# PEER's rows of u turned by VectorE in 32x32 squares, with plain fp32 products beside the picking and split products behind it

## The reference, cut to what matters

```python
def peer_ffn(h, q_w, sub_keys, u_tab, v_tab):      # h: 256 x 1024, u_tab, v_tab: 16384 x 1024
    q = (t @ q_w).reshape(n, 8, 2, 128)
    s = jnp.einsum('thpd,hpnd->thpn', q, sub_keys)           # 8 heads, 2 x 128 keys
    s1, i1 = lax.top_k(s[:, :, 0], 16)
    s2, i2 = lax.top_k(s[:, :, 1], 16)
    ...                                                      # 16 of the 256 sums of a head
    gates = jax.nn.softmax(top_s, axis=-1)
    act = jax.nn.gelu(jnp.einsum('chkd,cd->chk', u_tab[i_c], x_c))
    return jnp.einsum('chk,chkd->cd', g_c * act, v_tab[i_c])
```

## Time and profile before

| | us |
|---|---|
| median of 3 runs | 2324.53 |
| lowest and highest | 2319.58, 2325.33 |
| the profiled execution | 2319.86 |
| its span | 2318.1 |

### The profile page before, as it was taken

How to read it: one execution, slowest core, us unless ns; L and a number is a source line. 1 busy time by engine, 2 the same in 40 slices (tenths; PEclk the granted TensorE clock), 3 DMA queues, 4 the chain that set the end, 5 groups by cost and what they waited for, 6 DMA issues and landing times.

```text
span 2318.1 us, 37450 instructions
## 1 busy us (share of the span) xinstructions
PE 2145.5 (93%) x14407; PEld 1931.0 (83%) x14407; DVE 1409.6 (61%) x2315; ACT 1016.8 (44%) x1870; POOL 186.9 (8%) x217
## 2 busy tenths in 40 slices
PE   6999899878899999789999699999999999999997
PEld 6876788778788889778888599999999999777775
DVE  5435777677676752154434628997666654666665
ACT  4443443458553343233333424443444444555554
POOL 2101000001000000300000000000223341000000
PEclk9999999999999999879999899999999999999998
DMA  7543566734657743300001333343333335555553
GB/s 254 184 172 110 190 218 220 245 117 160 221 166 267 252 158 131 83 1 1 1 1 37 109 111 128 128 137 119 115 113 114 115 119 175 189 190 190 190 190 136
DMA packets 157432, 333.74 MB, mean 144 GB/s; under 512 B 17382, under 2 KB 69340, under 8 KB 157160
## 3 DMA queue, kind: packets, MB, share of 16 engines
q1 hardware_dynamic: 153896, 321.18, 41.0%
q0 software_dynamic: 3392, 10.52, 1.3%
HBM read 330.58 MB, written 1.08 MB: 143 GB/s over the span
## 4 chain that ended last, share of the span: by engine, by line
PE 73%; DVE 12%; PEld 7%; ACT 3%; issue 3%; SPq 1%; DMA 1%; PEldq 1%; DVEq 0%; ACTq 0%
PE psum L2130 18%; PE psum L2131 17%; PE psum L2132 17%; PE psum L2652 4%; PE psum L2699 2%; PEld psum L2130 2%; PEld psum L2131 2%; PEld psum L2132 2%; DVE weights_lo L1493 2%; PE psum L2542 2%; PE psum L2548 2%; DVE u_lo L2080 1%; PE psum L2523 1%; ACT weights_hi L1037 1%; PE psum L2428 1%
## 5 line engine op out<-in xcount | busy, mean ns | idle before, releaser
L1493 DVE TENSOR_TENSOR weights_lo<-weights,weights_hi 128x1024 fp32r<-128x1024 f32 (+2 forms) x336 | 345.3, 1085 | 260.4 <-ACT weights_hi L1037 255.3
L2130 PE MATMUL psum<-input_hi,weights_hi 128*128 128x256 f32 x1288 | 370.9, 288 | 19.0 <-DVE weights_lo L1493 6.1
L1037 ACT ACTIVATE weights_hi<-weights 128x1024 fp32r<-128x1024 f32 (+2 forms) x336 | 289.2, 931 | 178.7 <-PEq L2177 117.5
L2131 PE MATMUL psum<-input_lo,weights_hi 128*128 128x256 f32 x1288 | 367.1, 285 | 0.0
L2132 PE MATMUL psum<-input_hi,weights_lo 128*128 128x256 f32 x1288 | 366.9, 285 | 0.0
L2130 PE MATMUL psum<-input_hi,u_hi 128*128 128x256 f32 x1024 | 299.8, 293 | 0.0
L2132 PE MATMUL psum<-input_hi,u_lo 128*128 128x256 f32 x1024 | 289.3, 283 | 0.0
L2131 PE MATMUL psum<-input_lo,u_hi 128*128 128x256 f32 x1024 | 289.2, 282 | 0.0
L2130 PEld LDWEIGHTS psum<-input_hi,weights_hi 128*128 128x128 f32 x1288 | 250.0, 194 | 34.6 <-issue 32.7
L2080 DVE TENSOR_TENSOR u_lo<-psum,u_hi 128x512 fp32r<-128x512 f32 x256 | 164.8, 686 | 167.4 <-ACT u_hi L1419 165.9
L2131 PEld LDWEIGHTS psum<-input_lo,weights_hi 128*128 128x128 f32 x1288 | 250.0, 194 | 0.0
(11 more groups left out here) (376 smaller groups left out, 4001.4 us busy)
## 6 DMA issues: line engine op xcount, KB each, us to landing
u_rows<-in_peer_u_dram SPq DMA_DIRECT2D x128, 512.0 KB, 3.4
weights<-in_ffn_w_in_dram SPq DMA_DIRECT2D x44, 1024.0 KB, 7.3
v_rows_even<-in_peer_v_dram SPq DMA_DIRECT2D x64, 512.0 KB, 3.5
v_rows_odd<-in_peer_v_dram SPq DMA_DIRECT2D x64, 512.0 KB, 3.4
weights<-in_ret_w_in_dram SPq DMA_DIRECT2D x24, 1024.0 KB, 7.3
ada_rows_in<-in_ada_w_dram SPq DMA_DIRECT2D x24, 1024.0 KB, 5.2
weights<-in_ffn_w_out_dram SPq DMA_DIRECT2D x44, 512.0 KB, 6.5
weights<-in_lru_w_in_dram SPq DMA_DIRECT2D x12, 1024.0 KB, 6.3
```

Source lines behind the costliest of these rows:

```text
L1037: nc.scalar.activation(whi[:, r, at_], wraw[:, r, at_], ACT.Copy).then_inc(s_whi[r], 1)
L1493: ins = nc.vector.tensor_tensor(wlo[:, r, at_], wraw[:, r, at_], whi[:, r, at_].bitcast(F32), ALU.subtract)
L2130: nc.tensor.matmul(o, ah, bh, start=start, stop=False)
L2131: nc.tensor.matmul(o, ah, bl, start=False, stop=False)
```

## The change

SyncE loads a block of u in four DMAs of 32 rows each, so that partition 32a + e holds features 256a to 256a + 255 of row e; a transpose of every 32x32 square by VectorE then gives chunks of 128 features by 128 experts. A chunk k holds the features 256a + 32k + j, so the input of PEER is brought in the same order: `modulate` writes the second of its two instructions in that order, and the query weights' rows are loaded to match, one DMA for each chunk (8 a slot). TensorE's transposes of u are gone. For blocks 0 to 48 (`PARTED`) the turned rows go straight to plain fp32 products, 8 a block, with an unsplit input `HT` that GpSimd adds up from `HH` and `HL`; they use four buffers. From block 49 on ScalarE and VectorE split the turned rows, in one instruction of 1024 each, out of SBUF. The one-hot rows of both factors are made by one instruction, and the gate is multiplied into them by ScalarE (`gates_in`, four instructions) in place of VectorE.

```diff
+PARTED = GROUP_FIRST
+def plain_buffer(j):
+    return j % 4
+def parted(j):
+    return (j - PARTED) // 2 + 1
...
         UR = low.take("u_rows", [P, 2, D])
+        HT = Region("u's hi parts, before", low.at, 8 * KB).take("input_t", [P, KT, S])
         UTH = low.take("u_hi", [P, 2, KT, P], F32R)
+        UF2 = Region("u's lo parts, before", low.at, 8 * KB).take("u_turned_more", [P, 2, KT, P])
         UTL = low.take("u_lo", [P, 2, KT, P], F32R)
+        UT = Region("idle rows", rows_at, 8 * KB).take("u_turned", [P, 2, KT, P])
+        UF = [UT[:, 0], UT[:, 1], UF2[:, 0], UF2[:, 1]]
...
+                for k in range(KT):
+                    sp.dma_start(wraw[:, r, k * BANK:(k + 1) * BANK], q_rows[k, :, :, j * BANK:(j + 1) * BANK])\
+                        .then_inc(s_wload[r], 16)
...
-                sp.dma_start(UR[:, b, :], u_tab[bass.ds(i * 256 + j * P, P), :]).then_inc(s_ur[b], 16)
+                for c in range(4):
+                    four = u_tab[bass.ds(i * 256 + j * P + c * 32, 32), :].rearrange("e (a k) -> a e k", a=4)
+                    sp.dma_start(UR[:, b, c * 256:(c + 1) * 256], four).then_inc(s_ur[b], 16)
...
+                nc.gpsimd.tensor_tensor(HT[:, half, :], HH[:, half, :].bitcast(F32), HL[:, half, :].bitcast(F32), ALU.add)\
+                    .then_inc(s_ht, 1)
...
             def u_high(j):
+                if j < PARTED:
+                    return
+                b = j % 2
+                act.wait_ge(s_ut[b], j // 2 + 1)
+                act.wait_ge(s_ap, max(j - 1, PARTED))
+                nc.scalar.activation(UTH[:, b, :, :], UT[:, b, :, :], ACT.Copy).then_inc(s_uh[b], 1)
+
+            def gates_in(g):
+                act.wait_ge(s_oh, g + 1)
+                for x in range(4):
+                    one = ONE[:, g % 2, 0, x, :]
+                    t = 4 * g + x
+                    ins = nc.scalar.activation(one, one, ACT.Copy, scale=HKT[:, 2, t:t + 1])
+                ins.then_inc(s_ohg, 1)
...
                 if group_made(j - 2) is not None:
                     gates_out(group_made(j - 2), j + 1)
+                if group_made(j) is not None:
+                    gates_in(group_made(j))
...
+                if j < 2 and isinstance(i, int):
+                    act.wait_ge(s_ul[j], parted(P - 2 + j))
...
+            def turn_u(j):
+                b = j % 2
+                dve.wait_ge(s_ur[b], 64 * (j // 2) + 64)
+                if j < PARTED:
+                    dst = UF[plain_buffer(j)]
+                    if j >= 4:
+                        dve.wait_ge(s_ap, j - 3)
+                else:
+                    dst = UT[:, b]
+                    if j < PARTED + 2:
+                        dve.wait_ge(s_ap, max(m for m in range(j) if m < PARTED and plain_buffer(m) == b) + 1)
+                    else:
+                        dve.wait_ge(s_ul[b], parted(j - 2))
+                nc.vector.transpose(dst.rearrange("p k (c e) -> p c k e", c=4),
+                                    UR[:, b, :].rearrange("p (c k j) -> p c k j", c=4, k=KT)).then_inc(s_ut[b], 1)
+
             def u_low(j):
+                if j == 0:
+                    turn_u(0)
+                if j + 1 < P:
+                    turn_u(j + 1)
+                if j >= PARTED:
+                    b = j % 2
+                    dve.wait_ge(s_uh[b], parted(j))
+                    nc.vector.tensor_tensor(UTL[:, b, :, :], UT[:, b, :, :], UTH[:, b, :, :].bitcast(F32), ALU.subtract)\
                         .then_inc(s_ul[b], 1)
...
-                nc.vector.tensor_tensor(ONE2[:, half, :], iota, of(1), ALU.is_equal)
-                chain.done(nc.vector.tensor_tensor(ONE1[:, half, :], iota, of(0), ALU.is_equal))
-                nc.vector.tensor_tensor(ONE1[:, half, :], ONE1[:, half, :], of(2), ALU.mult).then_inc(s_oh, 1)
+                nc.vector.tensor_tensor(ONE[:, g % 2], iota, places, ALU.is_equal).then_inc(s_oh, 1)
...
+                if j < PARTED:
+                    pe.wait_ge(s_ut[b], j // 2 + 1)
+                    for k in range(KT):
+                        ins = nc.tensor.matmul(PS[:, 2 + b, 0:S], UF[plain_buffer(j)][:, k, :], HT[:, k, :],
+                                               start=k == 0, stop=k == KT - 1)
```

More of the change, by code:

```diff
@@ L355, with slot_loads @@
 GROUP_FIRST = len(PICKS) + 3
+PARTED = GROUP_FIRST
[3 more added lines that the diff above has]
+    return (j - PARTED) // 2 + 1
+def slot_loads(s0, use):
+    late = s0 - SLOTS["peer_q"]
+    return 32 * use + 32 if late < 0 else 32 * (use - late // 2) + 16 * KT * (late // 2 + 1)
 def group_made(j):
@@ L555, in first_and_second_block @@
         NS = Region("idle input", hh_at + 8 * KB, 8 * KB).take("na_scores", [P, 4, 512])
+        NP = Region("idle input", hh_at + 8 * KB, 8 * KB).take("scaled", [P, TT, D])
         NPT = Region("low-rank inputs", lora_at, 4 * KB).take("na_probs_t", [P, 2, 512])
@@ L639, in first_and_second_block @@
         s_oh = sem("s_oh")
+        s_ohg = sem("s_ohg")
+        s_ht = sem("s_ht")
         s_ur = [sem(f"s_ur{b}") for b in range(2)]
@@ L996, in _ @@
             load_rows(14, 18)
+            for u in range(4):
+                evacuated(UNITS["norm_p"] + u)
+            for j in (2, 3):
+                r, use = slot(SLOTS["peer_q"] + j)
+                pool.wait_ge(s_wlo[r], use + 1)
+            for h in range(2):
+                half = slice(4 * h, 4 * h + 4)
+                nc.gpsimd.tensor_tensor(HT[:, half, :], HH[:, half, :].bitcast(F32), HL[:, half, :].bitcast(F32), ALU.add)\
+                    .then_inc(s_ht, 1)
             def gate_block(j):
@@ L1553, in gain_row, with modulate @@
                 return dst
-            def modulate(src, scale):
+            def modulate(src, scale, turned=False):
                 shift = row()
+                lies = (lambda x: x.rearrange("p (a k j) -> p a k j", a=4, k=KT)) if turned else lambda x: x
                 for tt in range(TT):
                     inverse_rms(tt)
-                    chain.done(nc.vector.scalar_tensor_tensor(XS[:, tt, :], src[:, tt, :], rs[:, tt:tt + 1], scale,
+                    scaled = (NP if turned else XS)[:, tt, :]
+                    dst = XS[:, tt, :].rearrange("p (k a j) -> p a k j", a=4, k=KT) if turned else XS[:, tt, :]
+                    chain.done(nc.vector.scalar_tensor_tensor(scaled, src[:, tt, :], rs[:, tt:tt + 1], scale,
                                                               ALU.mult, ALU.mult))
-                    chain.done(nc.vector.tensor_tensor(XS[:, tt, :], XS[:, tt, :], shift, ALU.add))
+                    chain.done(nc.vector.tensor_tensor(dst, lies(scaled), lies(shift), ALU.add))
                     dve.sem_inc(s_xs, 1)
@@ L2089, in one_hot_rows @@
                     dve.wait_ge(s_gf, g - 1)
[L2090 to L2095 removed]
+                both = [P, 2, 4, P]
+                iota = IOTA[:, :].unsqueeze(1).unsqueeze(1).broadcast_to(both)
+                places = HKT[:, 0:2, 4 * g:4 * g + 4].unsqueeze(3).broadcast_to(both)
+                nc.vector.tensor_tensor(ONE[:, g % 2], iota, places, ALU.is_equal).then_inc(s_oh, 1)
             def beside(j):
@@ L2705, in _ @@
             pe.wait_ge(s_accfree, 10)
-            u_steps(turn_u, activations, beside)
+            pe.wait_ge(s_ht, 2)
+            u_steps(lambda *a: None, activations, beside)
             pe.wait_ge(s_hk, TT)
```

54 lines of the change are left out of this document (16 added, 38 removed).

## The result

The forecast was 2310.5 us, faster. The changed kernel takes **2509.09 us** in the median of four runs (2507.02 to 2519.13), against 2323.11 for the kernel before (four runs): a ratio of 1.081, 95% interval 1.078 to 1.084, 8% slower and far outside the range. The profiled execution has a span of 2507.7 us against 2318.1: 189.6 us more.

A forecast was written before the change was run, and what follows sets the result against it. Limits differ by part of the u stage: VectorE mostly beside the picking, TensorE beside the gates and in the last blocks. Gains 4 + 1 + 9 = 14 us give span 2304, 2310.5 us against the median; range 2278 to 2342.

The forecast's parts named there:

- what a load costs: Loads of u and query weights: 4.4 us a block, later ones hidden; weights 2.7 us of queue, costing nothing.
- A rival: u's smaller pieces land late, 6 us; last blocks lose their gain: 2325, no change; 0.12 shared with 1.35-1.6 us transposes.
- VectorE's transpose: One 128x1024 transpose a block in the u stage takes 1.20 us, the cost of the two low parts it replaces.
- The slow transpose: Rival: every element passes VectorE twice, 2.29 us a block, mostly costing beside the picking; 2367 us; chance 0.17.
- Beside the picking: Blocks 0 to 48, while VectorE does the picking steps: VectorE decides, its sum stays unchanged; gain 4 us.
- the gap before block 49: TensorE waits while VectorE does block 48's transpose (1.25), block 49's low parts (1.24) and some 0.2 handing over.
- The ring: Blocks 49 to 112: high parts, low parts, one-hot rows, scalings follow each other across ScalarE and VectorE, 4.65 us a round.
- fast ring: Rival beside the gates: scalings start every 0.21 us, round 4.33, gain 20 us more, 2290 us; chance 0.22.
- No ring: Rival beside the gates: TensorE's 3.85 us round, 50 us more gain, 2260; chance 0.05, shared with both cheaper.
- The mis-sized term: Beside the gates: VectorE's one-hot rows, 128x1024 with broadcast sources, take 1.21 us, as the first match instruction.
- start of the gates: Stretch beside the gates, blocks 49 to 112: 1 us of gain counted for the start.
- The last blocks: Last 15 blocks, without gates: TensorE's 2.95 us a round bounds; some 12 blocks gain 0.79 each, 9 us total.

The follow-up runs named there:

- both mended: Changed kernel with u's and the query weights' loads cut by quarters of the partitions (outermost dimension 32): 2325.84 us, ratio 1.0011 to the kernel before.
- the cut: Changed kernel with both loads cut by partition quarters, and ScalarE's four scalings called one block later, behind the next high parts: 2254.6 us, ratio 0.972 to the kernel before.
- N = 8: Kernel before with each u block's single load, 4 KB pieces, rearranged to outermost dimension 8: 2339.23 us.
- N = 16: Kernel before with each u block's single load, 4 KB pieces, rearranged to outermost dimension 16: 2322.95 us.
- N = 2: Kernel before with each u block's single load, 4 KB pieces, rearranged to outermost dimension 2: 3061.5 us.
- N = 4: Kernel before with each u block's single load, 4 KB pieces, rearranged to outermost dimension 4: 2432.12 us.

## Why the prediction was wrong, point by point

- **The step that failed: what a load costs.** "3.4 + 3 x 0.33 = 4.4 us" for a block, "Later loads have two rounds, over 6 us, and are hidden", and for the query weights "8 x 0.33 = 2.7 us of a queue that has nothing else to do there" and "Nothing there". I priced the new DMAs by the landing of a load with 128 partitions outermost, added the issues, and never asked what the new order of dimensions does to a transfer. A block's loads take 5.57 us, and since two buffers are refilled by one queue at that rate, no round is shorter: 81 + 89 us in the u stage. The weights cost 16 us.
- **A rival had the right suspect and the wrong mechanism.** It had the pieces of u landing late, at 6 us, and gave 2325. The landing was worse than its 6 us: SyncE starts to ask for the block turned at 1692.85 at 1683.24 us, 9.6 us earlier, with the other buffer's loads still on their way. I let it cost only the start and the last blocks. The condition that counts is the transfer's length against the round, 5.57 against 4.64 and 4.1: one transfer after another on the same few engines is a rate. The rate to hold it against was one division away: 128 blocks of 512 KB in 552.6 us are 121 GB/s. With 128 outermost the 1 KB pieces themselves cost nothing.
- **VectorE's transpose**: right, 1245 ns, 1.17 from start to start beside another instruction (taken: 1.20). The slow transpose is out. Of the two VectorE pages of the Trainium skill that were weighed, Vector Engine (DVE) Microarchitecture Reference agrees with the row; eight times the 311 ns of VectorE: DVE Perf Modes does not.
- **Beside the picking**: right once the loads are mended. Plain products 3.5 us a block; the gap before block 49 is 2.61 us, where the steps have 1.25 + 1.24 + 0.2 = 2.7. Last scores to block 49: 202.1 before, 196.7 with both mended, 5.4 gained (forecast 4).
- **The ring**: right, and seen only behind the mended loads. Four scalings 1.18 us (1.16), no cheaper for a plain copy, so the fast ring is out. No ring at all could be had by order alone, as that rival said. That its 2260 is near the 2254.6 measured is partly luck: it took 50 us off 2310.5, and the cut took 68.5 off a kernel of 2325.8.
- **The mis-sized term**: one-hot rows at 1.21 us, read from a match instruction beside the picking, where GpSimd does nothing (0.00 of 50 us). Beside the gates GpSimd works, and they take 1.37 at 1700 us and 1.73 at 1905, 1.46 in the mean. The rounds are 4.89 us in the mean (63 from 1600.35 to 1908.14), not 4.65: 15 us lost where the sum has 1 gained. "GpSimd's products are not in the ring" is true of the order and not of the time.
- **The last blocks**: with both mended, 45.8 us from the last gate products to v against 52.5 before: 6.7 gained, forecast 9.
- **Together**: for the change with sound loads the sum is -5.4 + 0.6 (start of the gates) + 15.5 - 6.7: 4 us lost instead of 14 gained, and GpSimd's 18 are the difference. What was wrong by the other 183 us (2509.1 - 2325.8) were the two rewritten loads (169 + 15 by stages), which I costed by their count and size alone.

What stays open: that the share of N/16 is N engines at work is inferred, and shown at 2 and 4 only; why N = 8 carries no more than 122 GB/s is not explained. The 1 KB against 4 KB piece at 4 outermost (94 against 104 GB/s) was not separated from the four issues, each of which also holds the queue longer there (547 ns against 317 with both mended).

## What to carry to other kernels

When a change rewrites a DMA's access pattern, look at its outermost dimension first, then at the bytes: compare the rate that the loop needs with the rate the window shows, and read a DMA share that stands still at a simple fraction (here 0.27, 0.13), while an engine waits for its rows, as a transfer that not all DMA engines carry, however low it looks. Take an instruction's price from a stage in which the same other engines are working. And a change that seems to lose can hold a gain behind a fault of its own: here 8% slower became 3% faster by mended loads and one call moved, and the second shows nothing without the first.

## What was unexpected of the hardware

- The DMA share can rise at equal work: with N = 16 outermost it was 0.49 at 125 GB/s, with 128 outermost 0.38 at 127, and the times were equal (2322.95 and 2323.11). The share alone does not tell how much is moved.
- GpSimd and VectorE slow each other both ways, and which of them pays goes, as far as the rows above tell, by which starts first. GpSimd's product of 452 columns takes 2.41 us when it starts under the one-hot rows, where before one of 448 took 1.42; the one-hot rows take 1.73 when they start under a product, and 1.22 without. That VectorE pays was tested by leaving the products out; GpSimd's side is read from timelines.
- In the waits of N = 2 TensorE's granted clock fell to 0.67 and 0.73 in the windows above, from 1.00: it stood idle 19 of 50 us and more. So a slow load costs products too: a transpose of u took 381 ns there in the mean, and 276 to 280 with N = 8 and N = 4, where the clock stayed at 1.00.
